# Attention probabilities as float16 pairs, turned by DMA instead of TensorE

## The reference, cut to what matters

```
# C: window attention, 4 query heads on 2 key heads, blocks of 128 queries see 256 keys, one sink per head
s = where(valid, q_c @ k_c.T * hd ** -0.5, -inf)
p = softmax(concat([s, sink]))[..., :-1]
c_out = (p @ v_c) * silu(s_z)
# D: memory attention, 4 heads, every query sees the same 256 memory tokens
p = softmax(q_d @ mem_k.T * hd ** -0.5)
d_out = (p @ mem_v) * silu(m_z)
# all four groups, per layer:  h = rmsnorm(x);  p = h @ w_in;  y = x + rmsnorm(concat(A, B, C, D) @ w_out)
```

## Time and profile before

| | us |
|---|---|
| median of 3 runs | 2154.7 (2153.5 to 2156.65) |
| the profiled execution's own time | 2150.82 |
| its span in the trace | 2148.7 |
| PE busy in the span | 2047.2 (95%) |
| DVE, ACT, POOL busy | 1230.9, 854.8, 336.8 |
| PE clock granted, mean | 0.981 of full |

### The profile page before, as it was taken

How to read it: one execution, slowest core, us unless ns; L and a number is a source line. 1 busy time by engine, 2 the same in 40 slices (tenths; PEclk the granted TensorE clock), 3 DMA queues, 4 the chain that set the end, 5 groups by cost and what they waited for, 6 DMA issues and landing times. The chain is left out here.

```text
span 2148.7 us, 43406 instructions
## 1 busy us (share of the span) xinstructions
PE 2047.2 (95%) x16698; PEld 1176.4 (55%) x16698; DVE 1230.9 (57%) x2763; ACT 854.8 (40%) x1981; POOL 336.8 (16%) x267
## 2 busy tenths in 40 slices
PE   9999899989999998998999998999999999989988
PEld 4455445545566665765445444454446666656633
DVE  5467755456367754544645785555553777644433
ACT  4544333444355332343435442344434543233322
POOL 1443323001000000000133343320010000000000
PEclk9999999999999999999999998999999999999999
DMA  7431223246311122223353232213552112122332
GB/s 265 131 99 40 81 79 99 89 136 212 119 41 32 55 68 75 77 82 138 133 145 99 70 85 84 84 54 109 186 190 63 60 32 72 47 80 65 91 118 88
DMA packets 192327, 208.13 MB, mean 97 GB/s; under 512 B 53462, under 2 KB 137948, under 8 KB 192092
## 3 DMA queue, kind: packets, MB, share of 16 engines
q1 hardware_dynamic: 189012, 194.77, 29.7%
q10 hardware_dynamic: 3112, 10.59, 1.6%
HBM read 136.60 MB, written 57.71 MB: 90 GB/s over the span
## 5 line engine op out<-in xcount | busy, mean ns | idle before, releaser
L1936 PE MATMUL bank<-h_hi,w_parts 128*128 128x512 f16 (+4 forms) x4240 | 839.8, 344 | 16.5 <-ACTq L2311 9.8
L1936 PEld LDWEIGHTS bank<-h_hi,w_parts 128*128 128x128 f16 (+1 forms) x4240 | 403.3, 98 | 358.6 <-issue 55.8
L1936 PE MATMUL bank<-h_lo,w_parts 128*128 128x512 f16 (+3 forms) x2160 | 440.2, 343 | 2.8 <-DVEq L2562 0.5
L1936 PEld LDWEIGHTS bank<-h_lo,w_parts 128*128 128x128 f16 (+1 forms) x2160 | 205.1, 98 | 174.9 <-issue 16.5
L3012 PE MATMUL bank<-scr_h,tb_h 128*128 128x512 f16 x768 | 179.4, 393 | 14.9 <-ACT tb_h L2332 9.1
L3012 PE MATMUL bank<-w_parts,tb_h 128*128 128x512 f16 x768 | 170.3, 379 | 1.6 <-DVEq L3160 1.6
L2310 ACT ACTIVATE tb<-bank 128x512 f32<-128x512 f32 (+1 forms) x140 | 71.3, 509 | 250.0 <-PE bank L1936 229.6
L2843 POOL TENSOR_SCALAR w_raw<-w_raw 128x1024 f32<-128x1024 f32 x46 | 130.8, 2848 | 82.9 <-DMA w_raw<-in_w_in 82.5
L3012 PEld LDWEIGHTS bank<-scr_h,tb_h 128*128 128x128 f16 x768 | 76.9, 101 | 109.1 <-issue 16.0
L2443 ACT ACTIVATE scr<-bank,stat 128x256 f32<-128x256 f32 x256 | 117.4, 470 | 34.0 <-DVE stat L2789 31.4
L2463 ACT ACTIVATE scr<-bank 128x1024 f32<-128x1024 f32 x64 | 65.5, 1023 | 164.0 <-PE bank L2207 163.7
(11 more groups left out here) (300 smaller groups left out, 2700.3 us busy)
## 6 DMA issues: line engine op xcount, KB each, us to landing
w_in_kept<-w_parts SPq DMA_DIRECT2D x104, 256.0 KB, 4.3
w_parts<-w_in_kept SPq DMA_DIRECT2D x104, 256.0 KB, 2.9
w_raw<-in_w_in SPq DMA_DIRECT2D x48, 512.0 KB, 4.1
out<-scr SPq DMA_DIRECT2D x32, 512.0 KB, 2.6
scr<-in_x_prompt SPq DMA_DIRECT2D x16, 512.0 KB, 4.2
scr<-out SPq DMA_DIRECT2D x16, 512.0 KB, 4.3
rot<-out ACTq DMA_DIRECT2D x12, 512.0 KB, 3.6
mix_t<-in_x_prompt SPq DMA_DIRECT2D x8, 512.0 KB, 11.9
```

Of the source, the lines that this page charges most:

```text
L1936: m = mm(bank[b][0:m_w, 0:c1 - c0], w[:, k, 0:m_w], h[:, k, c0:c1], start=it["piece"] == 0 and k == 0, stop=it["piece"] == 2 and k == KT - 1)
```

## The change

`turn` is gone for the prompt (the sample steps keep it). The exponentials are written back into their own bank. `scale` computes only the reciprocal, times 2^14. A new item `split_hi` (ACT) writes the scaled probabilities as float16 from the bank, `split_lo` (DVE) writes the float16 rest and then frees the banks. After each, SP issues one transposing DMA of 128x1024 float16 from `p` to `pt`, from SBUF to SBUF. The values are split alike (C in `rope_k`, one added DVE instruction; D once per layer). `value` makes three float16 products, 24 matmuls of 128 columns for C and 12 of 256 columns for D. The second pair has its own banks, 2 and 3, and its own buffers: for D in `rot`, for C in `scr` or, in second passes, in `w_raw`. The keys of C0 may be written to `rot` only when slots 0 and 1 have ended. The planner's costs follow. Cut to its core:

```diff
-PART_US = {"soft": 3.5, "scale": 1.4, "fac_exp": 1.1, "spread": 0.5, "held": 2.2}
+PART_US = {"soft": 3.5, "scale": 1.4, "fac_exp": 1.1, "spread": 0.5}
+HELD_US = {"soft": 6.1, "scale": 4.0, "split_hi": 3.7, "split_lo": 1.8}
-            st["key_after"] = last_window.get(st["st"], 0)
+            st["key_after"] = last_window.get(st["st"], 2)
...
-                out.append(item("score", [6, 7], step=s, c=c))
+                out.append(item("score", [2, 3] if c else [6, 7], step=s, c=c))
             for c in range(PAIRS) if not sample else ():
-                out.append(item("turn", [2, 3], step=s, c=c))
                 out.append(item("value", [4 + c], step=s, c=c, j=0))
...
+        elif kind == "scale" and it["step"]["st"] != "s":
+            parts.append((fc.at[("prob", n, c)], "ACT", item("split_hi", step=it["step"], c=c, of=it["of"])))
+        elif kind == "split_hi":
+            parts.append((fc.at[("prob_hi", n, c)], "DVE", item("split_lo", step=it["step"], c=c, of=it["of"])))
...
+                elif it["kind"] in ("split_hi", "split_lo"):
+                    s, c = it["step"], it["c"]
+                    j = int(it["kind"] == "split_lo")
+                    sp.wait_ge((prob_hi_done, prob_lo_done)[j], 1 + splits.index((s["n"], c)))
+                    sp.dma_start_transpose(prob_part(s, c, "pt", j).rearrange("p (x q) -> p x q", q=P), prob_part(s, c, "p", j)
+                                           ).then_inc(prob_turned[c], 16)
...
-                            for h in range(2):
-                                for i in range(2):
-                                    o = 2 * 256 * h + 256 * (b - 2) + P * i
-                                    m = nc.tensor.transpose(bank[b][:, (2 * h + i) * P:(2 * h + i + 1) * P], p[:, o:o + P], ident[:])
...
+                        pe.wait_ge(prob_turned[c], 2 * 16 * (1 + [x for x in splits if x[1] == c].index((s["n"], c))))
...
+                    terms = [(0, 0), (0, 1), (1, 0)]
                         for j in range(2):
                             for i in range(2):
+                                for vn, pn in terms:
+                                    for h in range(2):
+                                        v = v_prev[:, g, HD * vn:HD * vn + HD] if blk < 0 else value_part(s, vn)[:, blk, :]
+                                        m = mm(bank[b][HD * h:HD * h + HD, CH * j:CH * j + CH], v, pts[pn][:, h, j, i, :],
+                                               start=(i, vn, pn) == (0, 0, 0), stop=(i, vn, pn) == (1, 1, 0))
+                    elif s["st"] != "s":
+                        for i in range(2):
+                            for vn, pn in terms:
                                 for h in range(2):
+                                    m = mm(bank[b][HD * h:HD * h + HD, 0:2 * CH].rearrange("p (j q) -> p j q", j=2), mem_v[:, i, vn, o:o + HD],
+                                           pts[pn][:, h, i], start=(i, vn, pn) == (0, 0, 0), stop=(i, vn, pn) == (1, 1, 0))
...
-                    if not sample and it["c"] > 0:
-
-                        turn_read(act, s, it["c"] - 1)
...
                         for x in range(4):
-                            h, i = x // 2, x % 2
-                            m = fn(p[:, 256 * x:256 * x + 256], bank[6 + h][:, 256 * i:256 * i + 256], ACT.Exp, bias=z[:, 4 + x:5 + x],
+                            at = scores_of(it["of"], x)
+                            m = fn(at, at, ACT.Exp, bias=z[:, 4 + x:5 + x],
                                    scale=1.0 if unit == "C" else HD ** -0.5, accum_out=z[:, 12 + x:13 + x])
                         m.then_inc(exp_done, 1)
-                        act.drain().then_inc(bank_free[6], 1)
-                        act.drain().then_inc(bank_free[7], 1)
+                elif kind == "split_hi":
+                    for x in range(4):
+                        m = fn(hi[:, 256 * x:256 * x + 256], scores_of(it["of"], x), ACT.Copy, scale=z[:, 20 + x:21 + x])
+                    m.then_inc(prob_hi_done, 1)
...
-                        fn(pt.rearrange("p (b n) -> p b n", b=2), psum[:, 2:4, :], ACT.Copy).then_inc(bank_free[2], 1)
-                        act.drain().then_inc(bank_free[3], 1)
...
+                        dve.wait_ge(v_hi_done, 1 + v_splits.index(s["n"]))
+                        stt(value_part(s, 1), src, V_UP, value_part(s, 0), ALU.mult, ALU.subtract).then_inc(v_lo_done, 1)
+                        dve.drain().then_inc(bank_free[5], 1)
...
+                    if s["st"] != "s":
+                        link(ts(z[:, at_sum:at_sum + nh], z[:, at_sum:at_sum + nh], 1.0 / P_UP, None, ALU.mult))
+                        nc.vector.reciprocal(z[:, at_inv:at_inv + nh], z[:, at_sum:at_sum + nh]).then_inc(prob_done, 1)
+                        continue
+                elif kind == "split_lo":
+                    dve.wait_ge(prob_hi_done, 1 + splits.index((s["n"], c)))
+                    for x in range(4):
+                        m = stt(lo[:, part], scores_of(it["of"], x), z[:, 20 + x:21 + x], hi[:, part], ALU.mult, ALU.subtract)
+                    m.then_inc(prob_lo_done, 1)
+                    dve.drain().then_inc(bank_free[b0], 1)
+                    dve.drain().then_inc(bank_free[b0 + 1], 1)
...
+                        stt(mix_t[:, mix_row(s), c0:c0 + w], bank[b][:, 0:w], 1.0 / (P_UP * V_UP), z, ALU.mult, ALU.mult
+                            ).then_inc(bank_free[b], 1)
```

More of the change, by code:

```diff
@@ L151, with keeps_banks @@
 TABLE_US = 1.28
-def keeps_banks(soft):
-    return soft["step"]["unit"] == "D" or soft["step"]["st"] != "s"
+CHAIN = ("soft", "scale", "split_hi", "split_lo")
+def keeps_banks(part):
+    if part["kind"] == "soft":
+        return part["step"]["unit"] == "D" or part["step"]["st"] != "s"
+    return part["kind"] in CHAIN and part["step"]["st"] != "s"
 def banks_of(it):
@@ L280, in place @@
             p = run("PE", 0.27 if small else 0.6, self.needs(it))
-            self.free(run("ACT", 0.22 if small else 0.38, p), 5)
+            q = run("ACT", 0.22 if small else 0.38, p)
+            if not small:
+                at[("v", n)] = q = run("DVE", 0.45, q)
+            self.free(q, 5)
             at[("keyed", n)] = run("DVE", 0.55 if small else 1.95)
@@ L593, in emit @@
             n_scores[0] += 1
-            while any(x["kind"] in ("soft", "scale") and x["of"]["no"] <= it["no"] - STATS for _, _, x in parts):
-                emit_part("soft", "scale")
+            while any(x["kind"] in CHAIN and x["of"]["no"] <= it["no"] - STATS for _, _, x in parts):
+                emit_part(*CHAIN)
         elif kind == "turn":
             while ("scale", n, c) not in placed:
-                emit(parts.pop(next(i for i, x in enumerate(parts) if x[2]["kind"] in ("soft", "scale") and not behind_turn(x[2])))[2])
+                emit_part(*CHAIN)
+        elif kind == "value" and it["step"]["st"] != "s":
+            while ("split_lo", n, c) not in placed:
+                emit_part(*CHAIN)
         elif kind == "fac_prod":
@@ L658, in emit_part, with emit_parts @@
         emit(parts.pop(next(i for i, x in enumerate(parts) if x[2]["kind"] in kinds))[2])
[L660 to L666, removed]
+    def emit_parts(until=0.0):
         while True:
@@ L671, in emit_parts @@
             for when, eng, it in parts:
-                if it["kind"] not in kinds and not behind_turn(it) and when <= max(fc.t["PE"], fc.t[eng]):
+                if it["kind"] not in kinds and when <= max(until, fc.t["PE"], fc.t[eng]):
                     emit_part(it["kind"])
@@ L895, in plan_units @@
         it = queue.pop(0)
+        if when > now + EARLY:
+            emit_parts(when)
         if it["kind"] == "proj":
@@ L1533, in value_of, with value_part, prob_part @@
         def value_of(s):
-            return tok_v_s if s["st"] == "s" else tok_v[:, s["buffer"], :]
+            return tok_v_s
+        def value_part(s, j):
+            return tok_v[:, s["buffer"], :, j]
+        def prob_part(s, c, name, j):
+            o = 2 * ATT_P[name][0] + 2 * ST * j
+            if c == 0:
+                return scr_h[:, o:o + 2 * ST]
+            if s["unit"] == "D":
+                return rot_h[:, o:o + 2 * ST]
+            if second:
+                return w_raw_h[:, o:o + 2 * ST]
+            o += 2 * ATT_P["end"][0]
+            return scr_h[:, o:o + 2 * ST]
         def query_turned(s):
```

179 lines of the change are left out of this document (108 added, 71 removed).

## The result

The changed kernel took 2162.97 us (median of five, 2157.5 to 2167.4) where the kernel before took 2153.5 (five, 2146.8 to 2156.7): ratio 1.0049, interval 1.0032 to 1.0065. It is slower by half a per cent; 2094 was forecast, and the range ended at 2140.

A forecast was written before the change was run, and what follows sets the result against it. PE, busy 95% of the span, was taken to bound the kernel. 59.5 us (turns) + 10.2 (value products) gained, 3 (visits) + 7 (held banks, SP waits) lost: 59.7 off 2154.7, said as 2094; range 2065 to 2140.

The forecast's parts named there:

- Time shed by the turns: Prompt transposes on PE: 64 turns of 0.93 us each removed, 59.5 us gained.
- Value products: PE's value matmuls: D 0.77 us, C 0.97 us instead of 1.03, together 10.2 us gained; worst cases 25 us lost.
- rival 2: More gained: C products at 32 ns, one visit less, no new idle, shorter slots; 2068 us, chance 0.09.
- The estimate from the Trainium skill's load time: C value products: 53 ns per 64-column weight load; without overlap 1.28 us, sum 10 us higher.
- DVE and ACT: Softmax and split work: DVE 54 us more, ACT 33 us, at most 55; both lie under PE.
- The landing: Transposing DMA of 256 KB before the value products: L of 5 us taken, 2.9 and 7.9 as ends.
- Rival 3: Slower: transposing DMA lands late, slots set the pace, PE idles; at L = 13.5, 2214 us, chance 0.14.
- Does the latency stay under cover?: Attention slots, first score to last value: 14.5 + L in D, longer from L = 11.5; C 14.6 + L, from 8.0.
- I take 7 us ... ends 0 and 25: Loss of 7 us for banks held longer by the splits and a longer wait behind SP.
- The sum: Whole kernel: 59.5 + 10.2 us gained, 3 + 7 lost, 59.7 us in all.
- Rival 4: No effect: PE time shed comes back as idle in the recurrent slots, DVE chain as long as before; chance 0.04.
- signs listed for "wrong": Landing over 8 us, PE's waits naming the transposing DMA, or PE idle in a unit stage up over 10 us.

## Why the prediction was wrong, point by point

- **Time shed by the turns:** right. Doubling them costs 59 us, as 64 x 0.93 said. PE's busy time fell 64 us against 69.7, that is for turns and products together.
- **Value products:** right in D (0.78 us, 0.77 forecast). In C the size was rival 2's: 24 go from 372.20 to 373.18, exit to the projections included, and 48 from 396.95 to 398.59, so at most 34 ns each where 40 was taken.

```profile
396.95 0.36 PE L2285 MATMUL bank<-scr_h,v_prev 128*64 128x128 f16 x6
397.14 1.34 PE L2285 MATMUL bank<-scr_h,spare_h 128*64 128x128 f16 x42
398.59 0.60 PE L1987 MATMUL bank<-h_hi,w_parts 128*128 128x512 f16 x2
```

  The estimate from the Trainium skill's load time ("TensorE: Matmul & The Clock Gate", "LDWEIGHTS (loading the stationary operand)"), 53 ns each, is above the 34 that this trace shows for 64-column weights.
- **DVE and ACT:** right in size for a pair. Four `split_lo` take 1.65 us (1.70 forecast), four `split_hi` 1.58 (1.53). Over the kernel DVE is busy 36 us more (54 forecast) and ACT 23 (33). Wrong was the conclusion that they lie under PE at no cost: leaving out the low halves gained 19 us, the high ones 4 to 9 more.
- **The landing:** 3.3 us in the median, 3.0 to 7.4 over all 128, where 5 was taken. Rival 3 hung on 8 or more, so its trigger did not occur, though what it said would follow (the slots set the pace and PE idles) did, at the stage's end:

```profile
scr_h<-scr_h SPq DMA_TRANSPOSE x80, 3.3
```

  The Trainium skill ("Advanced Engine Details and Errata", "X-Bar Transpose (TRN2)") has transposing DMAs as fast as plain ones; 3.3 us beside 2.9 for a plain one of 256 KB agrees within 0.4.
- **"Does the latency stay under cover?":** this is the step that failed. It added up a pair's own operations (14.5 + L, so under 20 us) and set that against a slot of 26.0. Where projections lie between, the D slot takes 24.8 us, and the C slot that starts at 375.00 gets the values of both pairs from 396.95 on, at least 22.0 us later (22.6 before, 19.6 forecast). The steps are as long as forecast, but each engine takes its part of one list in order, and the chain goes through DVE once more and through SP, where it went through PE before. In the last D slot 4.0 of the 10.5 us from reciprocal to product are standing behind other work. And the cover itself was taken for granted: that last slot takes 20.0 us, near the forecast, but PE has no projections after 437.0 and stands 11.3 us, where it stood 0.4 before.
- **"I take 7 us ... ends 0 and 25":** the term that was mis-sized. Its measured size is 71 us of idle. The removal runs give 20 for the landing, 12 for SP and traffic, 19 and 4 to 9 for the splits, 56 to 60 in all. The sum had assumed that what PE sheds is time saved, since projections fill the gaps. The two kernels stripped of turning show 31 of some 47 and 48 of 78.5 us saved at these margins; the rest came back as idle.
- **Rival 4** (what PE sheds comes back as idle in the recurrent slots, chance 0.04) was nearest in time and partly right in mechanism: idle from 100 to 300 us, where the recurrent slots of the first stage lie, grew from 14.6 to 22.8 us, and one wait there is 7.0:

```profile
245.83 0.45 PE L2044 MATMUL bank<-ident,scr 128*128 128x128 f32 x1 [7.01 <-DVE scr L2704]
```

  But the last slot's 11 us, which it did not name, weigh more. No rival had a slower kernel with a short landing.
- **The range** left out any case in which the order of the items decides. Margins of some tenths of a microsecond turned out to be worth 42 us in the kernel before and 81 in the changed one, the latter more than any term of the sum. Two of the signs listed for "wrong" (PE's waits name the DMA, idle in a stage up by over 10 us) did show it.

What stays open: why `SAFE` and `EARLY` matter this much. The end of a stage shows where the time goes, not why slots fall behind by that amount; and the run with `TURN_US` alone at 0.3 went against what a shorter forecast should do. Seven settings of the changed kernel, its own included, and three of the kernel before don't show that the best one was found for either; that the change gains 1.4% rests on one pair of margins. Of the 73 us by which PE's idle grew in the four stages, about half ends with waits for the transposing DMAs; the rest, before evictions and in the recurrent units, was not taken apart.

## What to carry to other kernels

Before pricing a removal of work one for one, find where the work that should fill the gap ends, and follow one item through every queue it passes, with what stands ahead of it there and not only its own steps. A list of waits names whoever came last: removing that one (here the DMA) gave back 20 us and put DVE in its place, as the other engines' timelines of the same slot had shown. Where a planner writes the order, compare both kernels at re-tuned margins too: this change is 0.5% slower at the old ones and 1.4% faster at the one other pair tried in both.

## What the runs showed of the hardware

- A transposing DMA of 128x1024 float16 holds SP for 1.23 to 1.34 us in these rows (over all 128 the medians are 1.26 to 1.32, the longest 3.7), two plain ones of 256 KB for 1.65 together (SP in the changed kernel):

```profile
405.81 1.65 SPq L1822 DMA_DIRECT2D w_in_kept<-w_parts  x2
412.72 1.24 SPq L1850 DMA_TRANSPOSE scr_h<-scr_h  x1
...
415.46 1.34 SPq L1850 DMA_TRANSPOSE scr_h<-scr_h  x1
417.96 1.23 SPq L1850 DMA_TRANSPOSE rot_h<-rot_h  x1
```

  So 128 of them are an estimated 160 us of SP. The Trainium skill ("DMA: Bandwidth & Descriptors", "Issuing engines are not separate DMA queues") calls the time to start a DMA usually small beside the transfer; here it is over a third of the 3.3 us, and with the traffic it cost 7 to 12 us.
- The granted clock fell where PE had stood idle, and what followed took longer. Two stretches of the changed kernel around the last D slot (columns as in the earlier trace rows):

```profile
441.00:447.00 6.00, 1.28 (x12) 0.90 (x12) 4.48 (x10) 2.56 (x5) 0.00 (x0) 0.50 0.76 175
...
426.00:437.00 11.00, 10.89 (x58) 5.22 (x56) 7.17 (x12) 4.98 (x18) 0.00 (x0) 1.00 0.21 63
```

  Up to 437 PE was busy and had 1.00 (2.4 GHz). Then it stood idle for 8.7 us, the clock was 0.50 (1.2 GHz), and the 12 products took 1.49 us instead of 0.84. Over the whole kernel, the same 16314 matmuls were busy 1983.1, 1977.9, 1963.6 and 1955.2 us at mean clocks of 0.964, 0.966, 0.980 and 0.990 (changed kernel, with new costs, with new margins, with both): 28 of the 85 us between first and last are busy time, not idle. How much of the 28 is the clock stays open: with `TURN_US` alone at 0.3 the same matmuls were busy 1993.0 us at 0.964, and with `SAFE` 0.1 and `EARLY` 0.4 1982.0 us at 0.977.
